# One-hots of the second expert table: sixteen column one-hots on ScalarE as 8-bit tiles, two row one-hots ahead of the last dot products

## The chip, the cores and the metric

The kernel runs on one core of a Trainium2 chip. The metric is the device time of one execution in microseconds (us); a measurement is the median of several executions. Engines are named as the profile names them: PE is TensorE, ACT is ScalarE, DVE is VectorE, POOL is GpSimd and SP is SyncE. POOL and SP mainly issue DMAs here.

## The reference

One layer of a streaming encoder over 384 tokens: 256 prompt tokens (two tiles of 128, "tile 0" and "tile 1") and 128 stream tokens. After an input projection, two attention branches, a gated merge and a residual, a channel mixer (PEER) works on the normalized tokens. The change is in the mixer. Each token picks 16 experts for each of 8 heads out of 128 x 128 = 16384, that is 128 experts a token:

```python
idx  = i * 128 + j                     # top 16 of the sums of two halves' top 16
gate = softmax(best_s)                 # over the 16 of a head
a    = einsum("thkd,td->thk", peer_u[idx], xb)
act  = gelu(a) * gate
out  = einsum("thk,thkd->td", act, peer_v[idx])
```

peer_u and peer_v have 16384 rows of 2048 f32 values. All arithmetic is in f32.

## The kernel before

The two prompt tiles are computed after the stream tokens, at the end of the program, in these stages.

**Dot products.** For each of the 2 x 128 slots (k = 0 to 255) POOL gathers one row of peer_u per token (128 rows of 8 KB) and DVE multiplies and sums it with the tokens (`dot`, L1580). For tile 1 the gathers go round 6 buffers (`ring`); one of them is `spare[:, 0:D]`, another `work[:, 2D:3D]`. A gather waits until the dot that read its buffer before is done. The pick of tile 1's experts is cut into steps and put between the dots, one after each fourth.

**Output, first 1024 columns, by a dense table.** For each tile a table `[i, token, j]` of activations is made and multiplied with all of peer_v's first 1024 columns. The table of a tile is made in 32 groups of 4 tokens (`QUAD` = 4, `QUADS` = 32), numbered g = 0 to 31 for tile 0 and 32 to 63 for tile 1. For each group there are
- a column one-hot `hot_j` (512 columns: 4 tokens x 128), which is 1 where the slot's j equals the column, in `stage`, two slots;
- a row one-hot `hot_i`, the same for i, in `normed`, two slots;
- `hot_a`: the column one-hot times the activation, by ACT (`scaled`, L1144, four instructions), two slots;
- four matmuls `hot_a` x `hot_i` (`scatter`, L867) into one of two PSUM banks;
- the copy of that bank into the table by ACT (`place_table`, L1160).

For tile 0 ACT makes both one-hots itself, as relu(1 - |x - column|) (`distances`, L1124: Abs; `hots`, L1132 and L1134: Relu), beside the dots of tile 1. For tile 1 DVE makes them with a compare (`hots` on DVE, L1599 column, L1600 row) after its last dot. Semaphores: `j_hot`, `i_hot`, `a_hot`, `g_done` and `g_placed` count groups that have passed each step, over both tiles.

**Dense product** (`dense`, L879). Once all 64 groups are placed, PE multiplies both tables with 128 blocks of 128 rows of peer_v. SP loads the blocks (512 KB each, L403) into four buffers: `spare[:, 0:DC]`, `spare[:, DC:2DC]`, `spare[:, 2DC:3DC]` and a part of `work`.

**Output, last 1024 columns, by gathers.** For each of the 256 slots POOL gathers half a row of peer_v per token (4 KB x 128, L571) into one of five buffers and DVE adds it, times the activation, to the sum (`add_half`, L1610). In tile 1's group stage DVE does one add after each group's one-hots, then the rest.

The order on DVE is written out by hand: 256 dots, `prompt_acts(1)`, then for q = 0 to 31 `hots(q)` and `add_half(q)`, then `add_half` 32 to 255, then the sum of the dense part (L1637). The order on ACT: tile 0's groups, `gate_exps(2)`, `place_pair(1)` (tile 1's i and j, transposed, to SBUF), `prompt_gelu(1)`, tile 1's `scaled` and `place_table`. In its loop ACT does `scaled(q + 1)` ahead of `place_table(q)`.

P = 128, D = 2048, DC = 1024, SLOTS = 128.

Of the kernel before, what the change touches and what calls it, by code (L numbers as in the profile page):

```python
# [4 lines left out]

F32 = mybir.dt.float32
U32 = mybir.dt.uint32
ALU = mybir.AluOpType
ACT = mybir.ActivationFunctionType
AX = mybir.AxisListType.X  # L10

P = 128
D = 2048
# [16 lines left out]
SLOTS = PH * TOPK  # L30
# [3 lines left out]
DC = D // 2  # L34
QUAD = 4
QUADS = P // QUAD
UBUF = (8, 6)
# [3 lines left out]
CANDS = TOPK + (TOPK - 1) * FEW  # L41
VBUF = 5
VD = 4

HALVES = ((2, 1, 2, 1, 1), (1, 1, 2, 1, 1), (1, 1, 2, 1, 1), (1, 2, 2, 1, 0))
PICK_HALVES = (0, 1, 1, 0)
# [150 lines left out]
def build(nc, a):  # L197

    with ExitStack() as ctx:
# [11 lines left out]
        spare = sb("spare", [P, 3 * DC])  # L211
# [7 lines left out]
        work = bigr[:, 6 * D:9 * D]  # L219
        stage = sb("stage", [P, 2, CW])  # L220
# [29 lines left out]
        pairT = [fold[:, n * P:(n + 2) * P].rearrange("p (n s) -> p n s", n=2) for n in (6, 18)]  # L250
# [47 lines left out]
        def lay(F, xT, att, y, h, mixed, xn2, prob):  # L298
# [29 lines left out]
                     [rows[:, 2, :], rows[:, 3, :], xTs_flat, yTs[:, :]])  # L328
        ER = Prompt(sem, [spare[:, 0:D], work[:, 2 * D:3 * D]] + ES.urow + ES.vrow + [wflat[:, n, :] for n in range(NP)],
                    [yTr[:, n * DC:(n + 1) * DC] for n in range(4)] + [work[:, 2 * D + DC:3 * D]],  # L330
                    [spare[:, n * DC:(n + 1) * DC] for n in range(3)] + [work[:, 2 * D:2 * D + DC]], ES)
        table = [bigs[:, :].rearrange("p (i t) -> p i t", t=P), bigr[:, 0:8 * D].rearrange("p (i t) -> p i t", t=P)]
        hot_j = stage[:, :, :].rearrange("p b (q n) -> p b q n", q=QUAD)
        hot_i = normed[:, :, :].rearrange("p b (q n) -> p b q n", q=QUAD)
        hot_a = [at[:, 0:2 * CW].rearrange("p (b q n) -> p b q n", b=2, q=QUAD) for at in (xTr_flat, pwork)]

        def ring(k):

            t, n = divmod(k, SLOTS)
            return n % UBUF[0] if t == 0 else (0, 1, 8, 9, 10, 11)[n % UBUF[1]]  # L340

        def landed(k):

            return ER.u_base[ring(k)] + 16 * sum(ring(m) == ring(k) for m in range(k + 1))

        def last_dot(u, end=2 * SLOTS):
            return max(m for m in range(end) if ring(m) == u)
# [4 lines left out]
        @block.sync  # L352
        def _(sp):
            def chunk(n, pieces):

                for s, (w, k0, col) in enumerate(pieces):
                    sp.wait_ge(piece_done, NP * n + s + 1)
                    if not isinstance(n, int):
                        sp.sem_inc(sp_turn, 1)
                    src = w[k0 * P:(k0 + KP) * P, bass.ds(col, CW)].rearrange("(k p) c -> p k c", p=P)  # L360
                    sp.dma_start(wring[:, s, :, :], src).then_inc(w_loaded[s], 16)

            def full(w, col):

                return [(w, KP * s, col) for s in range(NP)]

            sp.dma_start(ln1s[:, :], a["ln1"]).then_inc(S.xT_loaded, 16)
            sp.dma_start(xTs[:, :, :], a["xTs"].rearrange("p (k n) -> p k n", k=KT)).then_inc(S.xT_loaded, 16)
            for F in (S, R):
                c0 = F.chunk0  # L370
                for G in range(2 * GROUPS):
                    br, g = G // GROUPS, G % GROUPS
                    for c in range(3):
                        chunk(c0 + 3 * G + c, full(a["w_in"], (3 * br + c) * WIDTH + g * CW))
                        if F is S and G == 0 and c == 0:
                            sp.dma_start(S.h, a["x"][2 * P:T, :].rearrange("(t p) d -> p t d", p=P)
                                         ).then_inc(S.x_loaded, 16)
                with sp.Fori(0, NCH) as i:
                    n = i * 3 + (c0 + GATES)
                    chunk(n, full(a["w_in"], GCOL + i * CW))  # L380
                    chunk(n + 1, full(a["w_in"], GCOL + D + i * CW))
                    chunk(n + 2, [(a["w_br_a"], 0, i * CW), (a["w_br_a"], KP, i * CW),
                                  (a["w_br_b"], 0, i * CW), (a["w_br_b"], KP, i * CW)])

                sp.wait_ge(F.y_copied, 2 * HEADS)
                sp.wait_ge(F.v_stored, 16 * 2 * GROUPS * F.n)
                sp.dma_start(F.h, a["x"][F.tiles[0] * P:(F.tiles[-1] + 1) * P, :].rearrange("(t p) d -> p t d", p=P)
                             ).then_inc(F.x_again, 16)
                with sp.Fori(0, NCH) as i:
                    chunk(i + (c0 + OUT), full(a["w_out"], i * CW))  # L390
                with sp.Fori(0, NCH) as i:
                    chunk(i + (c0 + PQ), full(a["w_pq"], i * CW))
            sp.wait_ge(ES.v_free, len(ES.vrow) + SLOTS)
            sp.dma_start(a["y"][2 * P:T, :], hs[:, :]).then_inc(y_stored, 16)
            for i in range(P):
                b = i % VD
                if i == 0:
                    sp.wait_ge(ER.u_free, last_dot(0) + 1)
                elif i == 3:
                    sp.wait_ge(ER.u_free, last_dot(1) + 1)  # L400
                elif i >= VD:
                    sp.wait_ge(ER.d_done, i - VD + 1)
                sp.dma_start(ER.dense[b], a["peer_v"][i * P:(i + 1) * P, 0:DC]).then_inc(ER.d_loaded[b], 16)  # L403
            for t in range(2):
                sp.wait_ge(ER.y_summed, 2 * (t + 1))
                sp.wait_ge(ER.v_free, SLOTS * (t + 1))
                sp.dma_start(a["y"][t * P:(t + 1) * P, :], R.h[:, t, :]).then_inc(y_stored, 16)
            sp.wait_ge(y_stored, 16 * TT)
# [484 lines left out]
        def _(act):  # L893
# [216 lines left out]
            def place_pair(t):  # L1110

                act.wait_ge(ER.pair_turned, t + 1)
                act.activation(pairT[t], ps[:, 6, 2 * t * P:(2 * t + 2) * P].rearrange("p (n t) -> p n t", n=2),
                               ACT.Copy).then_inc(ER.pair_placed, 1)
# [22 lines left out]
            def scaled(t, q):  # L1137

                g = QUADS * t + q
                act.wait_ge(ER.j_hot, g + 1)  # L1140
                if t:
                    act.wait_ge(ER.g_done, g - 1)
                for n in range(QUAD):
                    last = act.activation(hot_a[t][:, g % 2, n, :], hot_j[:, g % 2, n, :], ACT.Copy,  # L1144
                                          scale=ractT[:, t, q * QUAD + n:q * QUAD + n + 1])
                last.then_inc(ER.a_hot, 1)

            def prompt_gelu(t):

                act.wait_ge(ER.u_free, SLOTS * (t + 1))  # L1150
                act.activation(rdots[:, t, :], rdots[:, t, :], ACT.Gelu).then_inc(ER.gelu_done, 1)
                act.wait_ge(ER.act_turned, t + 1)
                act.activation(ractT[:, t, :], ps[:, 7, t * P:(t + 1) * P], ACT.Copy).then_inc(ER.act_placed, 1)
                act.wait_ge(ER.act_placed, t + 1)
# [22 lines left out]
                place_table(0, q)  # L1177
            gate_exps(2)
            place_pair(1)
            prompt_gelu(1)  # L1180
            scaled(1, 0)
            for q in range(QUADS):
# [6 lines left out]
        def _(dve):  # L1189
# [393 lines left out]
            def prompt_acts(t):  # L1583

                dve.wait_ge(ER.gelu_done, t + 1)
                dve.tensor_tensor(gates[t], rdots[:, t, :], gates[t], ALU.mult).then_inc(ER.acts_ready, 1)  # L1586

            def hots(q):

                g = QUADS + q  # L1590
                b = g % 2
                grid = iotaP[:, :].unsqueeze(1).to_broadcast([P, QUAD, P])

                def column(n):
                    return pairT[1][:, n, q * QUAD:(q + 1) * QUAD].unsqueeze(2).to_broadcast([P, QUAD, P])

                dve.wait_ge(ER.a_hot, g - 1)
                dve.wait_ge(ER.g_done, g - 1)
                dve.tensor_tensor(hot_j[:, b, :, :], column(1), grid, ALU.is_equal).then_inc(ER.j_hot, 1)  # L1599
                dve.tensor_tensor(hot_i[:, b, :, :], column(0), grid, ALU.is_equal).then_inc(ER.i_hot, 1)  # L1600

            def add_half(k):
# [11 lines left out]
            for k in range(2 * SLOTS):  # L1614
                dot(k)
                if k == SLOTS + 1:
                    finish_first()
                    prompt_acts(0)
                if k % 4 == 3 and len(stages) > 1:
                    stages.pop(0)()  # L1620
            for stage_ in stages:
                stage_()
            prompt_acts(1)
            dve.wait_ge(ER.pair_placed, 2)
            dve.wait_ge(ER.grid_made, 1)
            dve.wait_ge(ER.j_hot, QUADS)
            dve.wait_ge(ER.i_hot, QUADS)
            for q in range(QUADS):
                hots(q)
                add_half(q)  # L1630
            for k in range(QUADS, 2 * SLOTS):
                add_half(k)
# [81 lines left out]
```

## Time and profile before

| | |
|---|---|
| three runs, us | 2847.97, 2853.62, 2841.93 (median 2847.97) |
| the profiled execution, us | 2852.17, of which its span is 2850.3 |
| busy, share of the span | PE 74%, DVE 66%, POOL 43%, ACT 17% |
| DMA | 1047.10 MB, mean 367 GB/s |
| last stages, us from the span's start | dots of tile 1 to 2309.7; groups of tile 1 to 2389.1; dense product to 2830.5; last add to 2842.3 |

How to read it: the page gives busy time of each engine, the chain of waits that ended last, and groups of instructions by line. An instruction's duration includes some overlap with its neighbours on the same engine, so the distance from start to start can be shorter. PE shows two records for each f32 matmul of a group (x8 for four).

### The profile page before, as it was taken

The numbers are of one execution on the slowest core, as the hardware profiler recorded it, in microseconds if no ns is written. First come the engines' busy times: TensorE is split into PE (matmuls) and PEld (weight loads), VectorE is DVE, ScalarE is ACT, GpSimd is POOL, SyncE is SP. The second block draws the span as 40 slices with busy tenths as digits, with TensorE's granted clock in tenths as the row PEclk, the third lists the DMA queues.
The fourth block names the chain that finished last, engine by engine and source line by source line (L and its number), as shares of the span: only waits on it lengthen the run. The fifth ranks groups of instructions, "written<-read, shape, count | busy, mean of one in ns | idle before, by whom it ended". The sixth has DMA issues, their size and how long they took to land.

```text
span 2850.3 us, 19537 instructions
## 1 busy us (share of the span) xinstructions
PE 2110.5 (74%) x6070; PEld 1066.4 (37%) x6070; DVE 1879.8 (66%) x2631; ACT 473.7 (17%) x1107; POOL 1237.0 (43%) x855
## 2 busy tenths in 40 slices
PE   7999999999999998879899920000441048999997
PEld 3665544444545443334344410000331035444443
DVE  1122000296777767657575899999999998666666
ACT  1222100111222210000001000000993043000000
POOL 2000000023444445435443367777777865444444
PEclk9999999999999999999999965555555558999998
DMA  9777688989999999999999999999999988999999
GB/s 360 276 280 259 216 295 287 306 331 367 362 392 397 403 386 373 409 397 392 409 410 357 410 390 403 403 412 377 394 399 416 421 325 288 410 407 405 407 407 358
DMA packets 271464, 1047.10 MB, mean 367 GB/s; under 512 B 19856, under 2 KB 19856, under 8 KB 203280
## 3 DMA queue, kind: packets, MB, share of 16 engines
q0 software_dynamic: 113792, 697.85, 60.9%
q1 hardware_dynamic: 154880, 343.97, 33.2%
q10 hardware_dynamic: 2704, 4.21, 0.4%
q8 instruction: 43, 0.70, 0.1%
q14 instruction: 45, 0.37, 0.0%
HBM read 1036.50 MB, written 9.45 MB: 367 GB/s over the span
## 4 chain that ended last, share of the span: by engine, by line
PE 38%; DVE 26%; DMA 25%; issue 5%; POOL 4%; ACT 1%; SPq 0%; DVEq 0%; POOLq 0%; ACTq 0%
PE ps L590 33%; DMA yTr<-in_peer_v,fold 11%; DVE bigs L1580 7%; DVE bigr L1580 6%; DMA bigr<-in_w_br_a 4%; DVE hr L1610 3%; POOL bigr L561 3%; DMA bigr<-in_w_out 3%; DMA bigr<-in_w_in 2%; DMA bigs<-in_peer_v,idxnow 2%; DVE spare L1580 2%; DMA bigr<-in_peer_v,fold 1%; DVE pwork L1393 1%; PE ps L651 1%; DMA bigs<-in_peer_u,idxnow 1%
## 5 line engine op out<-in xcount | busy, mean ns | idle before, releaser
L590 PE MATMUL ps<-bigr 128*128 128x512 f32 x1920 | 859.3, 605 | 41.1 <-DMA bigr<-in_w_in 22.0
L590 PEld LDWEIGHTS ps<-bigr 128*128 128x128 f32 x1920 | 367.1, 194 | 493.4 <-issue 437.8
L514 POOL DMA_INDIRECT bigs<-in_peer_u,idxnow x128 | 224.9, 1757 | 556.8 <-DVE bigs L1527 537.8
L590 PE MATMUL ps<-bigr,bigs 128*128 128x512 f32 x896 | 408.1, 610 | 20.8 <-DMA bigr<-in_w_in 17.2
L1610 DVE SCALAR_TENSOR_TENSOR hr<-yTr,fold,hr 128x1024 f32<-128x1024 f32 x205 | 263.3, 1284 | 131.5 <-DMA yTr<-in_peer_v,fold 130.1
L1517 DVE SCALAR_TENSOR_TENSOR bigs<-bigs,acts 128x2048 f32<-128x2048 f32 x128 | 300.8, 2350 | 63.1 <-DMA bigs<-in_peer_v,idxnow 63.0
L1527 DVE SCALAR_TENSOR_TENSOR bigs<-bigs 128x2048 f32<-128x2048 f32 x128 | 293.0, 2290 | 67.0 <-DMA bigs<-in_peer_u,idxnow 65.9
L571 POOL DMA_INDIRECT yTr<-in_peer_v,fold x205 | 208.5, 1017 | 220.8 <-DVE hr L1610 212.5
L1580 DVE SCALAR_TENSOR_TENSOR bigr<-bigr 128x2048 f32<-128x2048 f32 x122 | 276.1, 2288 | 6.8 <-DMA bigr<-in_peer_u,fold 6.3
L561 POOL DMA_INDIRECT bigr<-in_peer_u,fold x122 | 238.1, 1952 | 51.3 <-issue 35.5
L590 PEld LDWEIGHTS ps<-bigr,bigs 128*128 128x128 f32 x896 | 171.3, 196 | 220.2 <-issue 213.4
L514 POOL DMA_INDIRECT bigs<-in_peer_v,idxnow x128 | 208.1, 1625 | 51.4 <-issue 39.6
L855 PE MATMUL ps<-ident,fold 128*128 128x128 f32 x2 | 0.9, 474 | 289.7 <-DVE fold L1586 289.7
L1580 DVE SCALAR_TENSOR_TENSOR bigs<-bigs,bigr 128x2048 f32<-128x2048 f32 x96 | 214.8, 2286 | 0.6
L561 POOL DMA_INDIRECT bigs<-in_peer_u,fold x96 | 171.6, 1787 | 62.7 <-issue 25.3
L879 PE MATMUL ps<-spare,bigs 128*128 128x512 f32 x384 | 182.1, 597 | 0.7 <-ACT bigr L1160 0.7
L879 PE MATMUL ps<-spare,bigr 128*128 128x512 f32 x384 | 180.4, 592 | 0.0
L1348 DVE TENSOR_TENSOR bigr<-ps,bigr 128x512 f32<-128x512 f32 x24 | 15.8, 688 | 212.3 <-PE ps L590 212.3
L849 PE MATMUL ps<-ident,fold 128*128 128x128 f32 x4 | 1.4, 448 | 197.0 <-DVE fold L1485 197.0
L867 PE MATMUL ps<-normed,bigr 128*128 128x128 f32 x256 | 65.5, 437 | 101.5 <-issue 93.6
L590 PE MATMUL ps<-bigr,yTr 128*128 128x512 f32 x256 | 117.2, 620 | 17.7 <-DMA bigr<-in_w_br_a 14.5
L500 POOL IOTA fold<- 128x128 f32 x1 | 0.2, 243 | 259.0 <-DVE stage L1372 259.0
(257 smaller groups left out, 2232.4 us busy)
## 6 DMA issues: line engine op xcount, KB each, us to landing
bigr<-in_w_in SPq DMA_DIRECT2D x160, 1024.0 KB, 9.5
spare<-in_peer_v SPq DMA_DIRECT2D x96, 512.0 KB, 6.8
bigr<-in_w_out SPq DMA_DIRECT2D x32, 1024.0 KB, 9.7
bigr<-in_w_pq SPq DMA_DIRECT2D x32, 1024.0 KB, 7.2
bigr<-in_w_br_a SPq DMA_DIRECT2D x16, 1024.0 KB, 9.7
bigr<-in_w_br_b SPq DMA_DIRECT2D x16, 1024.0 KB, 8.1
bigr<-in_peer_v SPq DMA_DIRECT2D x32, 512.0 KB, 6.7
bigr<-in_ckT_a POOLq DMA_DIRECT2D x2, 2048.0 KB, 9.9
```

Source lines behind the costliest of these rows:

```text
L514: pool.indirect_dma_start(row, None, table[:, :], bass.IndirectOffsetOnAxis(ap=col, axis=0)).then_inc(loaded, 16)
L561: pool.indirect_dma_start(ER.urow[u], None, a["peer_u"][:, :], bass.IndirectOffsetOnAxis(ap=eidx[t][:, s:s + 1], axis=0)).then_inc(ER.u_lo ...
L571: pool.indirect_dma_start(ER.vrow[k % VBUF], None, halves, bass.IndirectOffsetOnAxis(ap=hidx[:, t, s:s + 1], axis=0)).then_inc(ER.v_loaded ...
L590: last = mm(ps[:, bank + t, :], src[:, k0 + k, t * P:(t + 1) * P], wring[:, s, k, :], start=(k0 + k == 0), stop=(k0 + k == kt - 1))
L651: last = mm(out[:, b * SQ:(b + 1) * SQ], ckT[:, j, b, :], q_of(j, 0)[:, b * SQ:(b + 1) * SQ], start=(not br and b == 0), stop=True, **sk)
L867: last = mm(ps[:, 4 + b, n * P:(n + 1) * P], hot_a[t][:, b, n, :], hot_i[:, b, n, :], start=(n == 0), stop=True, **sk)
L879: last = mm(ps[:, 2 * t + c, :], table[t][:, i, :], ER.dense[b][:, c * CW:(c + 1) * CW], start=(i == 0), stop=(i == P - 1))
L1393: step(dve.max_index(x[:, lo:lo + 8], v_[:, lo:lo + 8], w))
L1517: dve.scalar_tensor_tensor(h, E.vrow[s], acts[:, s:s + 1], h, ALU.mult, ALU.add).then_inc(E.v_free, 1)
L1527: dve.scalar_tensor_tensor(E.urow[u], E.urow[u], 1.0, xn, ALU.mult, ALU.mult, accum_out=dots[:, s:s + 1]).then_inc(E.u_free, 1)
L1580: dve.scalar_tensor_tensor(ER.urow[u], ER.urow[u], 1.0, R.xn2[:, t, :], ALU.mult, ALU.mult, accum_out=rdots[:, t, s:s + 1]).then_inc(ER.u_ ...
L1610: dve.scalar_tensor_tensor(h, ER.vrow[v], gates[t][:, s:s + 1], h, ALU.mult, ALU.add).then_inc(ER.v_free, 1)
```

## The change

Column one-hots of tile 1's groups 0 to 15 (`EARLY` = 16) are made by ACT, right after `place_pair(1)` and ahead of `prompt_gelu(1)`, as 8-bit values: Abs into the two slots of `hot_i` (f32), then Relu into one of 16 slots of 512 bytes, eight in `stage` and eight in `spare[:, 2DC:]`. For groups 16 to 31 DVE still writes the column one-hots, also as 8-bit, into the eight slots in `stage`, now ahead of its wait for PE. `scaled` of tile 1 reads the 8-bit tiles. The row one-hots of groups 0 and 1 are made by DVE ahead of dot 250 (2 x 128 - 6). The row one-hots of the others stay in the loop. The third and fourth dense buffers change places; the third is waited for as the part of `work` was, the fourth until group 15 has been scaled.

```diff
+EARLY = 16
-                    [spare[:, n * DC:(n + 1) * DC] for n in range(3)] + [work[:, 2 * D:2 * D + DC]], ES)
+                    [spare[:, n * DC:(n + 1) * DC] for n in range(2)] + [work[:, 2 * D:2 * D + DC], spare[:, 2 * DC:]], ES)
+        early_j = [at.bitcast(U8).rearrange("p (b q n) -> p b q n", q=QUAD, n=P)[:, b, :, :]
+                   for at in (stage[:, :, :].rearrange("p b c -> p (b c)"), spare[:, 2 * DC:]) for b in range(EARLY // 2)]
+        def j_slot(q):
+            return early_j[q if q < EARLY else q % (EARLY // 2)]
 # SP, dense loads
+                elif i == 2:
+                    sp.wait_ge(ER.u_free, last_dot(1) + 1)
                 elif i == 3:
-                    sp.wait_ge(ER.u_free, last_dot(1) + 1)
+                    sp.wait_ge(ER.a_hot, QUADS + EARLY)
 # ACT, scaled
+                hot = j_slot(q) if t else hot_j[:, g % 2, :, :]
                 for n in range(QUAD):
-                    last = act.activation(hot_a[t][:, g % 2, n, :], hot_j[:, g % 2, n, :], ACT.Copy,
+                    last = act.activation(hot_a[t][:, g % 2, n, :], hot[:, n, :], ACT.Copy,
+            def early_distances(q):
+                if q >= 2:
+                    act.wait_ge(ER.j_hot, QUADS + q - 1)
+                for n in range(QUAD):
+                    last = act.activation(hot_i[:, q % 2, n, :], iotaP, ACT.Abs, scale=-1.0,
+                                          bias=pairT[1][:, 1, q * QUAD + n:q * QUAD + n + 1])
+                last.then_inc(ER.apart, 1)
+            def early_hot(q):
+                act.wait_ge(ER.apart, QUADS + q + 1)
+                act.activation(early_j[q], hot_i[:, q % 2, :, :], ACT.Relu, scale=-1.0, bias=1.0
+                               ).then_inc(ER.j_hot, 1)
             place_pair(1)
+            act.wait_ge(ER.pair_placed, 2)
+            early_distances(0)
+            for q in range(EARLY):
+                if q + 1 < EARLY:
+                    early_distances(q + 1)
+                early_hot(q)
             prompt_gelu(1)
 # DVE, hots
-                dve.wait_ge(ER.a_hot, g - 1)
+                if q >= EARLY:
+                    dve.wait_ge(ER.a_hot, g - (EARLY if q < EARLY + EARLY // 2 else EARLY // 2) + 1)
+                    dve.tensor_tensor(j_slot(q), column(1), grid, ALU.is_equal).then_inc(ER.j_hot, 1)
                 dve.wait_ge(ER.g_done, g - 1)
-                dve.tensor_tensor(hot_j[:, b, :, :], column(1), grid, ALU.is_equal).then_inc(ER.j_hot, 1)
                 dve.tensor_tensor(hot_i[:, b, :, :], column(0), grid, ALU.is_equal).then_inc(ER.i_hot, 1)
 # DVE, in the loop over the dots
+                if k == 2 * SLOTS - UBUF[1]:
+                    dve.wait_ge(ER.pair_placed, 2)
+                    dve.wait_ge(ER.grid_made, 1)
+                    dve.wait_ge(ER.j_hot, QUADS + EARLY)
+                    dve.wait_ge(ER.i_hot, QUADS)
+                    for q in range(2):
+                        hots(q)
 # DVE, the loop over the groups
             for q in range(QUADS):
-                hots(q)
+                if q >= 2:
+                    hots(q)
                 add_half(q)
```

## Rows read from the trace of the kernel before

**Rows 1.** Chain of waits in order of time: start us, us, what.
```profile
2174.98 6.64 DVE bigr L1580 x6
...
2399.45 10.41 DMA yTr<-in_peer_v,fold
```

**Rows 2.** Stretches: from:to, us, busy (count) by engine, PEclk, DMA share, GB/s.
```profile
2193.00:2310.00 117.00, 0.00 (x0) 0.00 (x0) 109.35 (x97) 1.86 (x3) 100.39 (x47) 0.50 1.01 419
2310.80:2389.10 78.30, 56.56 (x257) 48.95 (x257) 78.19 (x98) 56.71 (x161) 36.75 (x33) 0.65 0.75 241
...
2400.00:2800.00 400.00, 400.00 (x934) 177.10 (x933) 248.98 (x194) 0.00 (x0) 185.52 (x194) 1.00 1.03 407
```

**Rows 3.** Groups by line in 2310.8:2389.1: count | busy us, mean ns | idle before.
```profile
L867 PE MATMUL ps<-normed,pwork 128*128 128x128 f32 x256 | 56.1, 388 | 21.0 <-DVE normed L1600 13.0 <-issue 8.0
...
L1144 ACT ACTIVATE pwork<-stage,fold 128x128 f32<-128x128 f32 x128 | 40.9, 390 | 20.2 <-DVE stage L1599 20.1
L1610 DVE SCALAR_TENSOR_TENSOR hr<-yTr,fold,hr 128x1024 f32<-128x1024 f32 x27 | 34.7, 1284 | 0.1
L571 POOL DMA_INDIRECT yTr<-in_peer_v,fold x26 | 30.5, 1175 | 34.0 <-DVE hr L1610 34.0
```

**Rows 4.** Timeline of the group stage: start us, us, engine, line, operation [idle before].
```profile
2310.84 0.69 DVE L1599 TENSOR_TENSOR stage<-fold 128x512 f32<-128x512 f32 x1
2311.45 0.69 DVE L1600 TENSOR_TENSOR normed<-fold 128x512 f32<-128x512 f32 x1
2311.74 1.28 ACT L1144 ACTIVATE pwork<-stage,fold 128x128 f32<-128x128 f32 x4
2313.11 2.05 PE L867 MATMUL ps<-normed,pwork 128*128 128x128 f32 x8 [1.72 <-DVE normed L1600]
...
2384.95 1.13 PE L867 MATMUL ps<-normed,pwork 128*128 128x128 f32 x8 [1.27 <-DVE normed L1600]
2385.85 0.69 DVE L1600 TENSOR_TENSOR normed<-fold 128x512 f32<-128x512 f32 x1
...
2389.16 3.56 PE L879 MATMUL ps<-spare,bigs 128*128 128x512 f32 x4 [0.69 <-ACT bigr L1160]
```

**Rows 5.** Timeline of ACT: a group of tile 0, then tile 1's first work.
```profile
2006.02 0.57 ACT L1160 ACTIVATE bigs<-ps 128x512 f32<-128x512 f32 x1
2006.49 1.26 ACT L1124 ACTIVATE stage<-fold 128x128 f32<-128x128 f32 x4
2007.66 1.26 ACT L1124 ACTIVATE normed<-fold 128x128 f32<-128x128 f32 x4
...
2009.50 0.61 ACT L1134 ACTIVATE normed<-normed 128x512 f32<-128x512 f32 x1
...
2193.01 0.38 ACT L1113 ACTIVATE fold<-ps 128x256 f32<-128x256 f32 x1 [31.22 <-PE ps L849]
...
2309.80 0.31 ACT L1151 ACTIVATE fold<-fold 128x128 f32<-128x128 f32 x1 [115.11 <-DVE bigr L1580]
```

**Rows 6.** Timeline near the last dots: a dot and a gather's issue.
```profile
2295.02 2.29 DVE L1580 SCALAR_TENSOR_TENSOR bigr<-bigr 128x2048 f32<-128x2048 f32 x1 [0.19 <-DMA bigr<-in_peer_u,fold]
...
2295.94 2.19 POOL L561 DMA_INDIRECT bigr<-in_peer_u,fold  x1 [0.30 <-issue]
```

**Rows 7.** DMA issues, median us to landing, in 2320:2388, 2830:2845 and 2400:2800.
```profile
yTr<-in_peer_v,fold POOLq DMA_INDIRECT x22, 5.2
...
yTr<-in_peer_v,fold POOLq DMA_INDIRECT x4, 6.3
...
yTr<-in_peer_v,fold POOLq DMA_INDIRECT x155, 8.7
```

**Rows 8.** Timeline of the end: last dense matmuls, a gather's issue, the last add.
```profile
2828.60 1.88 PE L879 MATMUL ps<-bigr 128*128 128x512 f32 x4
2828.94 1.08 POOL L571 DMA_INDIRECT yTr<-in_peer_v,fold  x1 [0.31 <-issue]
...
2841.01 1.28 DVE L1610 SCALAR_TENSOR_TENSOR hr<-yTr,fold,hr 128x1024 f32<-128x1024 f32 x1
```

More of the change, by code:

```diff
@@ L7 @@
 U32 = mybir.dt.uint32
+U8 = mybir.dt.uint8
 ALU = mybir.AluOpType
@@ L1623, in _ @@
             prompt_acts(1)
[L1624 to L1627, printed above, removed]
             for q in range(QUADS):
-                hots(q)
+                if q >= 2:
+                    hots(q)
                 add_half(q)
```

## Prediction

> **What bounds the kernel now.** I read the chain of waits in order of time first, because the change touches only the end of the program. Until about 2310 us the chain runs through the dot products on DVE (three in 6.64 us, 2.21 each, where nothing holds them; x6 counts an accumulator read with each) and the gathers that feed them; from 2399 us to the end it is nothing but the gathers of half rows of peer_v into yTr and bigr, each with the add that reads it [rows 1]. Between these lies the stage that the change is about: the 32 groups of the second table (tile 1), from 2310.8 to 2389.1 us.
>
> The table of stretches [rows 2] gives each stage its limit. In 2193 to 2310 DVE is busy 109.35 of 117.00 us and the DMA engines are full (share 1.01), while ACT works 1.86 us and PE nothing. In the group stage of 78.3 us DVE is busy 78.19 us, ACT 56.71, PE 56.56, and the DMA engines carry 241 GB/s at a share of 0.75. From 2400 to 2800 us PE is busy 400.00 of 400.00 us and the DMA engines carry 407 GB/s at 1.03: two limits at once. The dense product ends near 2830.5 us, the adds end at 2842.3 us [rows 8].
>
> So the group stage belongs to DVE. The groups by line [rows 3] show its round: a column one-hot (L1599), a row one-hot (L1600) and one add (L1610). In the timeline the first row one-hot starts at 2311.45 and the last, the 32nd, at 2385.85 [rows 4]: 74.40 / 31 = 2.40 us a round. The first column one-hot starts 0.61 us before the row one-hot and the add takes the rest, so the round is 0.60 + 0.60 + 1.20, starts counted, with no gap. ACT scales a column one-hot in 1.28 us [rows 4] and copies a group out in 0.57 [rows 5]. PE takes 2.05 us for a group at 1.2 GHz and 1.13 us at 2.4 GHz [rows 4]; over the stage the granted clock is 0.65 [rows 2], and the 256 matmuls' 56.1 us [rows 3] are 1.75 us a group.
>
> **The change, part by part.** *16 column one-hots leave DVE.* For groups 0 to 15 DVE no longer writes L1599. Groups 16 to 31 keep it, as an 8-bit write placed ahead of the wait for PE.
>
> *ACT makes them early.* The work is four Abs of 128x128 and one Relu over 512 columns. On tile 0 four Abs take 1.26 us, next start after 1.17, and a Relu 0.61 [rows 5], so a group is about 1.17 + 0.60 = 1.8 us, and 16 of them 28 us. The place is behind place_pair(1), which ends at 2193.39. ACT's next real work is the Gelu at 2309.80, after 115.11 us of idleness [rows 5]. So the work ends near 2222 and 87 us of cover stay. The Gelu's table load moves behind it into the same gap. If this cover were gone, the whole 28 us would stand before the first group. Cost: 0.
>
> *Two row one-hots move ahead of dot 250.* That is 2 x 0.60 = 1.2 us of DVE, plus four waits that have long been met (the last, for ACT, near 2222). Behind it are the last six dots. Gathers for dots 250 to 255 wait only for dots 244 to 249, so no gather is issued later. Near the end a dot waits 0.19 us for its gather, and POOL issues a gather in 2.19 us with 0.30 between two, one each 2.49 us [rows 6]; DVE alone could start one each 2.21 [rows 1]. So 1.2 us of delay are paid off at 0.28 a dot over five gaps (1.4): cost 0, at most 0.3. If DVE had no slack there it would be 1.2.
>
> *The wait of SP.* SP now loads the third dense buffer after the last dot (a step of about 2.5 us) and the fourth only when group 15 has been scaled. Behind that wait on SP's queue stand the dense loads 4 on, and these wait for the first dense matmul anyway. The fourth load comes some 35 us before the stage ends. Cost 0; it even leaves the busy start of the stage.
>
> *The stage itself.* Group 0 isn't sooner: its matmul starts at 2313.11, when ACT's scaling that began at 2311.74 ends (2313.02) [rows 4]. Only DVE is ahead: the adds 0 and 1 are done by about 2313.3. Now row one-hot 2 is the first on DVE in the stage, and it needs group 0 read out of its slot (two slots): 2313.11 + 2.05 + 0.05 = 2315.2, where before it started at 2311.45 + 2 x 2.40 = 2316.25. That is 1.05 us (1.95 were PE at 2.4 GHz by then).
> For groups 2 to 15 DVE needs 0.60 + 1.20 = 1.80 us. The round of the other two engines is next: when group q-2 is done, ACT copies it out (next start after 0.48), scales group q (1.28), PE multiplies (2.05 or 1.13), with about 0.15 us of hand-overs. That is 3.95 us for two groups at 1.2 GHz, 1.98 each, and 3.0, 1.5 each, at 2.4 GHz. With the mean 1.75 it is 1.83. So the pace is 1.80 (PE fast) to 1.98 (PE slow), not 2.40. Over the 13 steps from group 2 to 15 DVE gains 13 x 0.60 = 7.8 or 13 x 0.42 = 5.5.
> Groups 16 to 31 have 0.60 + 0.60 + 1.20 again: 2.40, no gain and no loss, and PE and ACT catch up with DVE within two of them.
> Sum: 1.05 + 5.5 = 6.6 us with PE at 1.2 GHz, 1.05 + 7.8 = 8.9 with PE faster after group 0, 1.95 + 7.8 = 9.8 at the very best. Clock before in the stage is mixed (0.65), so I take 7.8.
>
> The Trainium skill ("TensorE: Matmul & The Clock Gate", Part 1) says that the low clock is the default state and that activity lifts it. By that rule a denser stream of groups stands at the upper end, 8.9 us. The trace agrees that both levels occur in this stage. It doesn't show the denser stream, so the sum above stays between.
>
> *8-bit tiles.* No row of the trace before writes or reads one. The nearest are the same operations on f32: 0.69 us for DVE's one-hot, 1.28 for ACT's four. From below, half of that (0.35) would save 16 x 0.34 = 5.5 us on groups 16 to 31; from above, double (1.38) would cost 16 x 0.69 = 11. I take the f32 rows, because the inputs of DVE's compare stay f32 and the count of elements stays 512.
>
> *What is late next.* The stage ends when the last group is copied out; then the dense product starts and lasts about 441 us, PE full from 2389.16 to 2830.5. The gathers: the stage issues one per round, so 32 before and 32 after. What is left behind it, bytes as well as matmuls, is the same, at the same 407 GB/s. So the gain reaches the end whole, if gathers keep up with 1.8 us. A landing takes 5.2 us in this stage, 6.3 in the tail and 8.7 in the dense stage [rows 7]; in the tail POOL issues one each 1.08 + 0.31 = 1.39 us [rows 8]. Five buffers give (1.28 + 0.1 + 5.2) / 5 = 1.32 us a gather, 2.0 with the 8.7.
>
> **The time.** 7.8 us off the profiled run's 2852.17 (span 2850.3) gives 2844.4. That run lies 4.2 us above the median of the three runs shown. Off the median, 2847.97 - 7.8 = 2840.2 us, and this is my forecast. It is 0.27%, under the 0.5% (14 us) that a measurement of this kernel can tell from no change; the three runs alone spread over 11.7 us.
>
> **Rivals.**
> 1. *The ring of ACT and PE takes DVE's place and PE stays slow*: 1.98 us a group, gain 6.6, 2841.4 us. For it: PE comes from 117 us without work [rows 2], and the mean of 1.75 us lies nearer to 2.05 than to 1.13. Against: groups of 1.13 us occur as well.
> 2. *The gathers hold the adds.* With landings of 8.7 us the pace is 2.0, gain 1.05 + 13 x 0.4 = 6.3. POOL's issue could also grow: 1.18 us in this stage [rows 3], 2.19 beside dots [rows 6]. At 2.19 + 0.30 = 2.49 a gather, the adds of the whole stage would be bound at 2.49 once the five landed rows are used: 27 x 2.49 + 5 x 1.8 = 76 against 77, a gain of about 1, 2847 us. Against: the tail issues one every 1.39 us beside the same adds. The Trainium skill ("SBUF — State Buffer", Who interferes with whom) says that a VectorE instruction with two SBUF inputs contends with a GpSimd instruction that reads SBUF. By that rule a denser DVE lengthens the issue here, at worst to the 2847 us just worked out; the trace shows both lengths beside such instructions.
> 3. *Slower: the 8-bit column one-hots on DVE cost more.* Place: L1599 of groups 16 to 31, on the path with no gap. The point from which it decides is 7.8 / 16 = 0.49 us more each, 1.18 instead of 0.69; at double, 1.38, it is 11 - 7.8 = 3 us slower than before, 2851.
> 4. *The gain isn't passed on*, because the adds end 12 us after the dense product and the DMA engines are full: 2848. Against: the bytes left when the dense product starts don't change, and the engines had room (0.75) before.
> 5. *The change doesn't do what it says*: ACT late. It would need over 115 us for what rows give 28.
>
> **How the numbers follow.** Forecast (a gain of 7 to 10 us) 0.55; rival 1 0.17; rival 2 0.10; rival 4 0.08; rival 3 0.04; rival 5 0.01; a one-hot in half the time (gain 13) 0.05. All but parts of the last and of rival 3 lie within 14 us of before, and the spread of runs moves some across: faster by over 0.5% 0.08, within 0.89, slower 0.03. The range goes from 2840.2 - 9 (the cheap 8-bit one-hot, or the fastest runs) to 2849 (no gain, and the spread): 2831 to 2849.
>
> **What would show it.** ACT busy about 30 us more in 2193 to 2225. Two one-hots of 0.69 just ahead of the sixth last dot, with the first group's scaling within 0.3 us of 2311.7. Row one-hots 1.8 to 2.0 us apart in groups 2 to 15 and 2.4 after. A stage of 70 to 71 us in place of 78.3. The dense product 441 us long, the last add 12 us after it. The forecast is wrong if L1599 with 8-bit output isn't 0.69, if adds wait for yTr within the stage, or if the dense stage grows by what the stage before it lost.

## The result and the profile after

| | before | changed |
|---|---|---|
| first comparison, median of 7 and 7 runs, us | 2852.75 (2833.9 to 2861.2) | 2833.29 (2830.4 to 2838.8) |
| ratio, 95% interval | | 0.9942 (0.9922 to 0.9963) |
| the changed kernel again, median of 12 runs (before: 32), us | 2845.91 (2836.5 to 2861.4) | 2839.81 (2830.2 to 2847.1) |
| ratio, 95% interval | | 0.9970 (0.9952 to 0.9988) |
| profiled execution / span, us | 2852.17 / 2850.3 | 2836.92 / 2835.0 |

The forecast was 2840.2 us, a gain of 7.8. By the ratios the first comparison shows 0.58% (16.5 us) and the second, which the experiments needed, 0.30% (8.5 us); their intervals overlap between 0.9952 and 0.9963. The quotients of the medians are 0.9932 and 0.9979, a sign of how far whole times scatter. The two profiles lie 15.3 us apart. The first task is therefore to find which part of this belongs to the change.

The stretches of the changed kernel that answer to [rows 2] (from:to, length, busy (count) of PE, PEld, DVE, ACT and POOL, PEclk, DMA share, GB/s):

```profile
2187.20:2303.00 115.80, 0.00 (x1) 0.00 (x0) 109.70 (x99) 30.32 (x82) 97.30 (x47) 0.50 1.01 418
2303.00:2373.50 70.50, 48.44 (x257) 41.81 (x257) 68.42 (x85) 55.73 (x162) 47.73 (x33) 0.76 0.81 273
...
2384.00:2784.00 400.00, 400.00 (x934) 177.10 (x933) 248.37 (x194) 0.00 (x0) 189.49 (x194) 1.00 1.02 407
```

ACT now works 30.32 us in the stretch in which it worked 1.86. The group stage, counted from the end of the last dot to the first dense matmul, is 70.5 us; in the kernel before it is 2389.16 - 2309.77 = 79.4. The dense stage is as full as it was.

The same moments in both profiles, us. "Stage" is counted as just said; "tail" is from the start of place_pair(1), which is the last thing ahead of the change, to the end of the last add:

| kernel | place_pair(1) | to last dot's end | stage | first dense matmul to last add | tail |
|---|---|---|---|---|---|
| before | 2193.0 | 116.8 | 79.4 | 453.1 | 649.3 |
| changed | 2187.2 | 115.8 | 70.5 | 453.5 | 639.8 |

Of the 15.3 us, 5.8 had been gained before anything of the change ran. The tail is 9.5 us shorter: 8.9 in the stage, 1.0 in the dots behind place_pair(1), 0.4 given back behind the stage. The 1.0 is no part of the change that I can show: this time is 115.3 to 117.7 us in the ten profiles.

ACT's early work, answering to [rows 5], and the last dots, answering to [rows 6] (timeline: start us, us, engine, line, operation, idle before):

```profile
2187.24 0.38 ACT L1123 ACTIVATE fold<-ps 128x256 f32<-128x256 f32 x1 [31.21 <-PE ps L859]
2187.65 2.44 ACT L1164 ACTIVATE normed<-fold 128x128 f32<-128x128 f32 x8
2190.01 0.61 ACT L1171 ACTIVATE stage<-normed 128x512 uint8<-128x512 f32 x1
2190.65 1.28 ACT L1164 ACTIVATE normed<-fold 128x128 f32<-128x128 f32 x4
2191.84 0.61 ACT L1171 ACTIVATE stage<-normed 128x512 uint8<-128x512 f32 x1
...
2216.79 1.28 ACT L1177 ACT_TABLE_LOAD   x1
...
2288.26 2.29 DVE L1612 SCALAR_TENSOR_TENSOR bigr<-bigr 128x2048 f32<-128x2048 f32 x1 [0.19 <-DMA bigr<-in_peer_u,fold]
...
2290.48 1.29 DVE L1633 TENSOR_TENSOR normed<-fold 128x512 f32<-128x512 f32 x2
2291.69 2.31 DVE L1612 SCALAR_TENSOR_TENSOR bigr<-bigr 128x2048 f32<-128x2048 f32 x1
...
2300.71 2.29 DVE L1612 SCALAR_TENSOR_TENSOR bigr<-bigr 128x2048 f32<-128x2048 f32 x1
2303.04 0.31 ACT L1177 ACTIVATE fold<-fold 128x128 f32<-128x128 f32 x1 [84.97 <-DVE bigr L1612]
```

A group takes 1.83 us (2190.01 to 2191.84), and 85 us of cover are left before the Gelu. The two row one-hots stand behind dot 250, not ahead of it as I had read the loop: `dot(k)` comes first in it, and the block that makes them follows. Five dots follow, from 2291.69 to 2300.71 in four steps, 2.26 us each instead of 2.49. Dot 250 started at 2288.26; at 2.49 us a dot the last would have started at 2288.26 + 5 x 2.49 = 2300.71, and that is when it did. The 1.2 us are paid off in full.

The group stage, answering to [rows 4]; the first line is row one-hot 2 of the kernel before, the rest is the changed kernel:

```profile
2316.25 0.69 DVE L1600 TENSOR_TENSOR normed<-fold 128x512 f32<-128x512 f32 x1
```
```profile
2304.97 2.44 ACT L1155 ACTIVATE pwork<-stage,fold 128x128 f32<-128x128 uint8 x8
2306.35 3.72 PE L877 MATMUL ps<-normed,pwork 128*128 128x128 f32 x16 [1.72 <-issue]
2308.43 0.69 DVE L1633 TENSOR_TENSOR normed<-fold 128x512 f32<-128x512 f32 x1 [1.74 <-PE ps L877]
2309.04 1.28 DVE L1643 SCALAR_TENSOR_TENSOR hr<-yTr,fold,hr 128x1024 f32<-128x1024 f32 x1
2310.24 0.69 DVE L1633 TENSOR_TENSOR normed<-fold 128x512 f32<-128x512 f32 x1
2310.29 1.13 PE L877 MATMUL ps<-normed,pwork 128*128 128x128 f32 x8 [0.22 <-issue]
2311.96 1.13 PE L877 MATMUL ps<-normed,pwork 128*128 128x128 f32 x8 [0.55 <-issue]
...
2331.80 0.70 DVE L1633 TENSOR_TENSOR normed<-fold 128x512 f32<-128x512 f32 x1
2332.40 1.29 DVE L1643 SCALAR_TENSOR_TENSOR hr<-yTr,fold,hr 128x1024 f32<-128x1024 f32 x1
2333.60 0.70 DVE L1631 TENSOR_TENSOR stage<-fold 128x512 uint8<-128x512 f32 x1
2334.20 0.70 DVE L1633 TENSOR_TENSOR normed<-fold 128x512 f32<-128x512 f32 x1
```

Row one-hot 2 starts 2308.43 - 2303.00 = 5.43 us after the last dot's end, where it was 2316.25 - 2309.77 = 6.48: the forecast's 1.05. From there to row one-hot 15 (2331.80) are 13 steps in 23.37 us, 1.80 each. Row one-hot 16 follows after 2.40. DVE's only wait of note is the 1.74 us before row one-hot 2.

### The profile page after: what moved, and what is told of

The parts are those of the page before. It is cut to its first block, busy times and chain, and to the rows that moved or that the text cites. A ratio compares the mean times of both kernels' runs of the same rounds, so it can differ in the third digit from the quotient of the medians.

```text
span 2835.0 us, 19569 instructions
## 1 busy us (share of the span) xinstructions
PE 2098.1 (74%) x6070; PEld 1056.1 (37%) x6070; DVE 1870.1 (66%) x2615; ACT 500.9 (18%) x1187; POOL 1254.9 (44%) x855
## 4 chain that ended last, share of the span: by engine, by line
PE 39%; DVE 25%; DMA 24%; POOL 5%; issue 5%; ACT 1%; POOLq 0%; SPq 0%; DVEq 0%; ACTq 0%
PE ps L600 34%; DMA yTr<-in_peer_v,fold 12%; DVE bigs L1612 7%; DVE bigr L1612 6%; DMA bigr<-in_w_br_a 4%; DVE hr L1643 3%; POOL bigr L571 3%; DMA bigr<-in_w_out 2%; DMA bigs<-in_peer_v,idxnow 2%; DVE spare L1612 2%; DMA bigr<-in_w_in 2%; DVE pwork L1425 1%; PE ps L661 1%; PE ps L718 1%; DVE bigs L1549 1%
## 5 line engine op out<-in xcount | busy, mean ns | idle before, releaser
L524 POOL DMA_INDIRECT bigs<-in_peer_u,idxnow x128 | 230.7, 1802 | 551.1 <-DVE bigs L1559 531.8
L1643 DVE SCALAR_TENSOR_TENSOR hr<-yTr,fold,hr 128x1024 f32<-128x1024 f32 x205 | 263.5, 1286 | 136.8 <-DMA yTr<-in_peer_v,fold 134.4
L1559 DVE SCALAR_TENSOR_TENSOR bigs<-bigs 128x2048 f32<-128x2048 f32 x128 | 293.0, 2290 | 63.8 <-DMA bigs<-in_peer_u,idxnow 62.4
L581 POOL DMA_INDIRECT yTr<-in_peer_v,fold x205 | 219.6, 1071 | 207.0 <-DVE hr L1643 197.6
```

The source lines that it names most:

```text
L524: pool.indirect_dma_start(row, None, table[:, :], bass.IndirectOffsetOnAxis(ap=col, axis=0)).then_inc(loaded, 16)
L581: pool.indirect_dma_start(ER.vrow[k % VBUF], None, halves, bass.IndirectOffsetOnAxis(ap=hidx[:, t, s:s + 1], axis=0)).then_inc(ER.v_loaded ...
L1559: dve.scalar_tensor_tensor(E.urow[u], E.urow[u], 1.0, xn, ALU.mult, ALU.mult, accum_out=dots[:, s:s + 1]).then_inc(E.u_free, 1)
L1643: dve.scalar_tensor_tensor(h, ER.vrow[v], gates[t][:, s:s + 1], h, ALU.mult, ALU.add).then_inc(ER.v_free, 1)
```

## The experiments

All kernels' profiles, in the measure of the table above:

| kernel | ratio (95%) | place_pair(1) | to last dot's end | stage | dense to last add | tail |
|---|---|---|---|---|---|---|
| null_before | 1.0006 (0.9988 to 1.0023) | 2179.4 | 117.7 | 80.3 | 454.4 | 652.4 |
| after_again | 0.9970 (0.9952 to 0.9988) | 2189.5 | 115.3 | 71.1 | 453.6 | 640.0 |
| early31 | 0.9946 (0.9923 to 0.9968) | 2187.7 | 116.1 | 62.4 | 452.3 | 630.8 |
| early8 | 0.9991 (0.9973 to 1.0009) | 2184.0 | 116.4 | 76.3 | 453.7 | 646.4 |
| no_ahead | 0.9980 (0.9963 to 0.9997) | 2192.1 | 116.2 | 70.9 | 451.4 | 638.5 |
| ahead_only | 0.9998 (0.9981 to 1.0014) | 2201.0 | 116.4 | 79.0 | 452.8 | 648.2 |
| no_cover | 1.0059 (1.0038 to 1.0080) | 2185.8 | 116.5 | 100.8 | 455.7 | 673.0 |
| ring_alone | 1.0092 (1.0057 to 1.0126) | 2196.4 | 116.3 | 56.9 | 502.8 | 676.0 |

The ratios of the first four are against 32 runs of the kernel before (median 2845.91 us), those of the last four against 22 others (median 2848.51 us). The last five columns come from one profile each.

### Is the start of the program part of the gain?

> The kernel before, unchanged, against itself. The question: in the pair of profiles shown, place_pair(1) starts 5.8 us earlier in the changed kernel (2187.24 against 2193.01), in code that the change doesn't touch. Theory A, chance: the first 500 us end at another time in each execution; then the ratio here is 1.000 within 0.003, place_pair(1) starts anywhere within some 6 us of 2193, and from it to the end of the last add it is 649.3 us within 1. Theory B, the change moves the start too: place_pair(1) of this kernel stays at 2193 within 1 us.

> The changed kernel, unchanged. From the start of place_pair(1) to the end of the last add 639.8 us within 1 by both theories (649.3 before). Theory A (only the end of the program is faster, by 9.4 us; the rest of the 15 to 19 us is chance): ratio 0.9967, place_pair(1) anywhere within some 6 us of 2190. Theory B (7 us come from ahead of place_pair(1) and belong to the change): ratio 0.994, place_pair(1) within 1 us of 2187.

place_pair(1) in the profiles of null_before and of ahead_only, whose code up to there is the same:

```profile
2179.42 0.38 ACT L1113 ACTIVATE fold<-ps 128x256 f32<-128x256 f32 x1 [31.21 <-PE ps L849]
```
```profile
2201.00 0.38 ACT L1113 ACTIVATE fold<-ps 128x256 f32<-128x256 f32 x1 [31.21 <-PE ps L849]
```

Theory A holds, except for its size. The ten profiles have place_pair(1) anywhere from 2179.4 to 2201.0, a spread of 21.6 us, with no order between kernels; the expected 6 us were too few. The 5.8 us between the first two profiles lie within what identical code shows, so they are put down to chance. They were there long before the change: the same instruction of DVE (L1365, L1397 in the changed kernel) starts at 513.36 us in the first profile and at 507.62 us in the second. The tail is what can be compared from single profiles: 649.3 and 652.4 for the kernel before, 639.8 and 640.0 for the changed one, whose 639.8 had been expected. null_before's 652.4 misses the expected 649.3 within 1: 0.9 of it are in the last dots, 0.9 in the stage and 1.3 behind it. In the stage, PE was at 1.2 GHz in the last group (2.05 us instead of 1.13), and this group ends the stage.

### The number of column one-hots: none, 8, 16, 31

```diff
-EARLY = 16
+EARLY = 31                      # early8: EARLY = 8, slots early_j[q % 16]
 ...
+        early_j += [at.bitcast(U8).rearrange("p (q n) -> p q n", q=QUAD) for at in
+                    [pwork[:, (8 + n) * P:(9 + n) * P] for n in range(3)] + [gates_s[:, :], eidx_s[:, :]]
+                    + [fold[:, n * P:(n + 1) * P] for n in (0, 1, 2, 3, 6, 7, 12, 17, 8, 4)]]
-                    sp.wait_ge(ER.a_hot, QUADS + EARLY)
+                    sp.wait_ge(ER.a_hot, QUADS + 16)       # early8: QUADS + QUADS
 ...
```

In early8 the fourth dense buffer is thus loaded only once the last group has been scaled, since its slots are in use until then; the time from the first dense matmul to the last add (453.7 us) shows no cost of that.

> ACT makes the column one-hots of groups 0 to 30 early (EARLY = 31; the added slots lie in pwork, gates_s, eidx_s and in blocks of fold that are free by then); DVE makes the last. Theory: DVE's round sets the stage, 1.80 us without a column one-hot and 2.40 with. Then groups 2 to 30 go at 1.80 and the stage from the end of the last dot to the first dense matmul, 79.4 us before and 70.5 in the changed kernel, is about 61.6 us; from place_pair(1) to the last add 631 us, ratio to the kernel before 0.9937 if nothing else moves. Rival: PE falls back to 1.2 GHz and the round of ACT and PE takes over, 1.98 us a group: the later groups gain 0.42 each, the stage is 64 us. Second rival: POOL's issue (1.50 us mean in the stage after, 1.94 at times) or the five row buffers hold the adds: DVE waits for yTr within the stage, which is then over 64 us.

> ACT makes only the column one-hots of groups 0 to 7 early (EARLY = 8, sixteen slots as before). Theory: 0.60 us for each column one-hot that leaves DVE from group 2 on and 1.05 for the first two together: the stage is 79.4 - 1.05 - 6 x 0.60 = 74.7 us, ratio about 0.998. Rival: the gain is due to the faster clock of PE or to the slots, not to the number of one-hots; then the stage stays near 70.5 us or near 79.4.

The stage of early31 as one stretch, its groups by line (count | busy, mean ns | idle before), and three steps late in it:

```profile
2303.80:2366.20 62.40, 39.92 (x257) 33.80 (x257) 60.23 (x69) 55.77 (x162) 39.53 (x33) 0.91 0.88 309
```
```profile
L1647 DVE SCALAR_TENSOR_TENSOR hr<-yTr,fold,hr 128x1024 f32<-128x1024 f32 x28 | 35.8, 1277 | 0.3
L585 POOL DMA_INDIRECT yTr<-in_peer_v,fold x26 | 31.7, 1220 | 18.5 <-DVE hr L1647 18.2 <-issue 0.3
L1637 DVE TENSOR_TENSOR normed<-fold 128x512 f32<-128x512 f32 x30 | 20.5, 682 | 1.7 <-PE ps L881 1.7
L1190 ACT ACTIVATE bigr<-ps 128x512 f32<-128x512 f32 x32 | 19.0, 594 | 3.4 <-PE ps L881 2.7
```
```profile
2343.41 0.68 DVE L1637 TENSOR_TENSOR normed<-fold 128x512 f32<-128x512 f32 x1
2344.01 1.28 DVE L1647 SCALAR_TENSOR_TENSOR hr<-yTr,fold,hr 128x1024 f32<-128x1024 f32 x1
2345.20 0.68 DVE L1637 TENSOR_TENSOR normed<-fold 128x512 f32<-128x512 f32 x1
```

DVE keeps 1.80 us a group to the end and waits 1.7 us in all; the adds don't wait for gathers (0.3). The tail is 630.8 us, expected 631. Both rivals fall: granted clock 0.91, not back at 0.50, and no wait for yTr. early8 gave 76.3 us instead of the 74.7 expected. One part is my count: row one-hots 3 to 7 are five steps, not six, so the sum is 79.4 - 1.05 - 5 x 0.60 = 75.35, as the row one-hots of its trace have it (number 8 starts 16.8 us after the last dot's end, 4.05 earlier than before). The other 0.9 are PE's clock in the last group, which ends the stage. The last group and the first dense matmuls of early8, and then of the changed kernel:

```profile
2373.95 2.05 PE L877 MATMUL ps<-normed,pwork 128*128 128x128 f32 x8 [0.35 <-issue]
2376.68 1.98 PE L889 MATMUL ps<-spare,bigs 128*128 128x512 f32 x4 [0.69 <-ACT bigr L1186]
```
```profile
2371.70 1.13 PE L877 MATMUL ps<-normed,pwork 128*128 128x128 f32 x8 [0.36 <-issue]
2373.52 1.98 PE L889 MATMUL ps<-spare,bigs 128*128 128x512 f32 x4 [0.69 <-ACT bigr L1186]
```

2.05 against 1.13 us: 0.92. early31's last group took 2.04 us too, which makes its 61.6 into 62.5 (62.4 measured). The last row one-hot isn't touched by that clock: it starts 76.1 us after the last dot's end before, and 72.0, 67.2 and 58.2 us after it with 8, 16 and 31 early column one-hots. The steps are 4.1 (1.05 + 5 x 0.60 = 4.05), 4.8 (8 x 0.60) and 9.0 (15 x 0.60). So the first three column one-hots are worth 1.05 us together and each later one 0.60 us.

early31 is faster than the kernel before: 2832.37 us, median of 9, against 2845.91, and 2839.81 for the changed kernel in the same comparison. Against the changed kernel the intervals of the ratios overlap, so whole times don't show a gain; the tail (630.8, one profile, against 639.8 and 640.0) does.

### What is the second part, the two row one-hots ahead, worth?

no_ahead is the changed kernel with the block in the loop over the dots taken out; its four waits stand ahead of the loop over the groups:

```diff
 ...
-                if q >= 2:
-                    hots(q)
+                hots(q)
                 add_half(q)
```

> The changed kernel without its second part: the row one-hots of groups 0 and 1 are made in the loop over the groups again, after the last dot. Theory: they were worth nothing. DVE with both in the loop is free 3.6 us after its start (2 x 0.60 + 2 x 1.20), the first group leaves PE 4.4 us after it, and row one-hot 2 waits for that in either kernel. So the stage stays at 70.5 to 71.1 us, and place_pair(1) to the last add at 640 us within 1. Rival: each is worth its 0.60 us, the stage is 1.2 us longer and the last dot 1 us earlier after place_pair(1) than in the changed kernel.

ahead_only is the kernel before with both one-hots of groups 0 and 1 behind dot 249:

```diff
+                if k == 2 * SLOTS - UBUF[1] - 1:
+                    ...                          # the four waits, moved here
+                    for q in range(2):
+                        hots(q)
 ...
             for q in range(QUADS):
-                hots(q)
+                if q >= 2:
+                    hots(q)
                 add_half(q)
```

> The kernel before, with both one-hots of groups 0 and 1 (four of 0.60 us) ahead of dot 250 and nothing early on ACT. Theory: 2.4 us of delay at dot 250, of which 1.4 are paid off before the last dot; row one-hot 2 comes 1.05 us earlier against the last dot; all others at 2.40. Stage about 78.4 us, place_pair(1) to the last add 649.3 within 1, ratio 1.000. Rival: the gain of the change lies in what is ahead of the last dots; then the stage is 4 us or more shorter.

Nothing that shows. no_ahead has a stage of 70.9 us and a tail of 638.5, a little outside the expected 640 within 1 and on the side that speaks against the rival. Its row one-hot 2 starts 5.43 us after the last dot's end, as in the changed kernel: DVE waits for group 0 either way (0.74 us here, 1.74 there). So the first 1.05 us of the gain come from column one-hots, not from the row one-hots.

ahead_only has 79.0 and 648.2, and a ratio of 0.9998. The expectation of 78.4 was 0.6 too low: its row one-hot 2 starts 6.11 us after the last dot's end, 0.4 earlier than before and not 1.05. The order in the code says why. The kernel before waits for group 0 ahead of column one-hot 2, so this one-hot (0.60) stands between the wait and row one-hot 2. The 1.05 us thus need the column one-hots of groups 0, 1 and 2 away from DVE.

### The cover, and the round of ACT and PE

```diff
             place_pair(1)
-            (early work)
             prompt_gelu(1)
+            (early work)
 ...
```

> The changed kernel with ACT's early column one-hots behind the Gelu of tile 1 instead of ahead of it (and the row one-hots in the loop, as in no_ahead, since they would otherwise wait for ever). The cover of the dots is gone. Theory: all of ACT's 16 x 1.83 = 29 us stand before the first group; stage 100 us, place_pair(1) to the last add 669 us, ratio about 1.007. Rival: the gathers that land meanwhile and the dense loads soften it, since the stage isn't full of transfers; it can't, as DVE adds nothing in that time and only five rows and three dense blocks have a buffer: under 660 us would speak for it.

```profile
2302.30:2332.00 29.70, 0.48 (x1) 0.18 (x1) 1.00 (x6) 27.85 (x80) 0.94 (x1) 0.50 0.22 86
```

In these first 29.7 us of no_cover's stage only ACT works and the transfers are at 86 GB/s. The stage is 100.8 us (100 expected), the tail 673.0 (669): all of ACT's work lies in the open once the dots no longer cover it. The rival falls. Of the 4 us too many 2.2 lie behind the stage, where the profiles but ring_alone's scatter from 451.4 to 455.7 us anyway.

ring_alone:

```diff
-                add_half(q)
-            for k in range(QUADS, 2 * SLOTS):
+                if q < 2:
+                    add_half(q)
+            for k in range(2, 2 * SLOTS):
```

> The changed kernel with the adds of slots 2 to 31 moved from the loop over the groups to behind it. It measures the round of ACT and PE alone, which was said to be 1.5 us a group with PE at 2.4 GHz and 1.98 at 1.2 GHz, and whether a shorter stage reaches the end when its gathers don't move along. Theory: DVE has 0.60 or 1.20 us of work a group, so ACT's 0.48 + 1.17 = 1.65 us is the pace of all groups: stage 2.4 + 32 x 1.65 = 56 us, 14 shorter than in the changed kernel. But 30 gathers more are left behind it, and the last add comes later: in the dense product's 440 us some 215 are done, then 39 at 1.39 us are left; last add 495 us after the first dense matmul (453.6 in the changed kernel), 667 us after place_pair(1), slower than both kernels. Rival (the stage alone counts): 626 us.

Stretches of ring_alone: the stage, the dense product, what is left behind it; and two of ACT's rounds:

```profile
2312.70:2369.60 56.90, 38.31 (x257) 32.91 (x257) 36.88 (x55) 53.67 (x162) 5.60 (x4) 0.93 0.19 75
2369.60:2810.00 440.40, 439.73 (x1024) 194.48 (x1024) 276.21 (x216) 0.00 (x0) 212.88 (x216) 1.00 1.02 402
2812.00:2870.00 58.00, 0.00 (x0) 0.00 (x0) 43.43 (x35) 0.00 (x0) 43.03 (x33) 0.50 0.89 307
```
```profile
2329.70 0.59 ACT L1186 ACTIVATE bigr<-ps 128x512 f32<-128x512 f32 x1
2330.18 1.28 ACT L1155 ACTIVATE pwork<-spare,fold 128x128 f32<-128x128 uint8 x4
2331.35 0.60 ACT L1186 ACTIVATE bigr<-ps 128x512 f32<-128x512 f32 x1
```

The round of ACT is 1.65 us (2329.70 to 2331.35), and ACT is the limit: 53.67 of 56.90 us busy. The stage is 56.9 us, 56 expected. Yet the last add comes 502.8 us after the first dense matmul instead of 453.6, and the kernel is slower than both others. The stage moved 75 GB/s instead of 273, and its 30 gathers came due behind the dense product, where 35 adds took 58 us, 1.66 each. I had taken 1.39 each; that explains the 8 us by which 495 was too low (39 x 1.66 = 65, 440 + 65 = 505, against 502.8).

## Why the prediction was right

*What bounds the stage, and by how much each column one-hot shortens it*: right. DVE had no gap at 2.40 us a group and has none at 1.80 (the timeline of the changed kernel), and the last row one-hot of early8, the changed kernel and early31 comes earlier by 0.60 us for each further column one-hot. By the prediction's own count, from the moment 1.08 us behind the last dot at which the first column one-hot used to start, 78.3 us became 69.4, just under its 70 to 71.

*The clock*: the term that was mis-sized. I took 7.8 between 6.6 (PE at 1.2 GHz) and 8.9 (PE faster after group 0); the stage gave 8.9. Group 0 still took 2.05 us, and from group 2 to group 15 PE took 1.13 to 1.16 us a group. The granted clock of the stage is 0.76 against 0.65, and it divides at row one-hot 16 (two stretches of the changed kernel):

```profile
2304.00:2334.00 30.00, 20.18 (x129) 17.22 (x129) 28.14 (x32) 26.73 (x80) 17.98 (x17) 0.90 0.88 315
2334.00:2373.50 39.50, 28.26 (x128) 24.58 (x128) 39.38 (x49) 28.68 (x81) 29.02 (x17) 0.65 0.74 238
```

The rule of the Trainium skill ("TensorE: Matmul & The Clock Gate", Part 1), that activity lifts the clock from its low default, was weighed and not followed; the trace agrees with it here, with 0.90 over the rounds of 1.80 us and 0.65 over those of 2.40. So rival 1 didn't come about. The round of ACT and PE at the high clock was mis-sized as well: I had 1.5 us, half of a chain over two groups, but ACT alone needs 0.48 + 1.17 = 1.65 us for each group, as ring_alone shows. That is still under DVE's 1.80, so the sum isn't touched. In early31 the high clock held through all the groups at 1.80 us.

*The cover*: right; 28 us were estimated, 16 x 1.83 = 29 are in the trace, and no_cover shows their price without it, 100.8 - 70.9 = 29.9 us in the stage against no_ahead, its nearest kernel.

*The two row one-hots*: cost 0, right. But their gain was stated together with that of the column one-hots; no_ahead shows that it is 0. The place was misread by one dot (they stand behind dot 250), with no effect on the sum: 1.2 us were paid off over the five dots that follow.

*The gain passed on whole*: right. 453.1 us from the first dense matmul to the last add before, 453.5 after, 452.3 in early31. The dense product itself takes 439.7 us where 441 were forecast, and the last add ends 13.8 us after it, not 12: the gathers and adds end the program, not PE. ring_alone shows the condition under which it holds: the stage must keep its gathers.

*Gathers and POOL's issue (rival 2)*: the adds didn't wait (0.2 us in all for L1643), though POOL's issue did grow, from 1.18 to 1.50 us in the mean:

```profile
L581 POOL DMA_INDIRECT yTr<-in_peer_v,fold x26 | 38.9, 1497 | 18.6 <-DVE hr L1643 18.3 <-issue 0.3
L1643 DVE SCALAR_TENSOR_TENSOR hr<-yTr,fold,hr 128x1024 f32<-128x1024 f32 x27 | 34.8, 1290 | 0.2
L1155 ACT ACTIVATE pwork<-stage,fold 128x128 f32<-128x128 uint8 x96 | 30.4, 390 | 11.5 <-DVE stage L1631 11.5
...
L1631 DVE TENSOR_TENSOR stage<-fold 128x512 uint8<-128x512 f32 x16 | 11.3, 704 | 0.0
```

The mean hides where. A round of the kernel before, then of the changed kernel a round of 1.80 us and one of 2.40:

```profile
2344.45 0.69 DVE L1599 TENSOR_TENSOR stage<-fold 128x512 f32<-128x512 f32 x1
...
2344.81 1.14 POOL L571 DMA_INDIRECT yTr<-in_peer_v,fold  x1 [1.26 <-DVE hr L1610]
```
```profile
2321.38 1.14 POOL L581 DMA_INDIRECT yTr<-in_peer_v,fold  x1 [0.66 <-DVE hr L1643]
...
2345.59 0.70 DVE L1631 TENSOR_TENSOR stage<-fold 128x512 uint8<-128x512 f32 x1
2345.96 1.75 POOL L581 DMA_INDIRECT yTr<-in_peer_v,fold  x1 [0.66 <-DVE hr L1643]
```

A denser DVE doesn't lengthen the issue here: it takes 1.14 us in the rounds of 1.80 us as in those of 2.40 before, and early31, dense to the end, has a mean of 1.22. The issue takes 1.75 us only in the rounds whose column one-hot DVE writes as 8-bit, at the same distance behind that one-hot (0.37 us) as before (0.36). I had derived the growth from the contention that the Trainium skill describes ("SBUF — State Buffer", Who interferes with whom) between a VectorE instruction with two SBUF inputs and a GpSimd instruction that reads SBUF. The trace doesn't bear this out: the one-hots and adds of the 1.80 us rounds are such instructions too. Why the 8-bit rounds are slower for POOL stays open, and other neighbours lengthen the issue as well (1.93 us at the end of the stage, beside adds alone). The price is hidden here because POOL still waits 0.66 us a round.

*8-bit tiles (rival 3)*: 0.70 us for DVE's 8-bit one-hot where f32 took 0.69, and 390 ns for ACT's scaling of one, as before [rows 3]. The choice of the f32 rows was right for these two engines; POOL's issue beside the 8-bit one-hots, 0.61 us longer, was a cost that the prediction didn't name.

*The size over all*: the forecast of 2840.2 stands against medians of 2833.29 and 2839.81. The first ratio is past the 0.5% to which I had given 0.08; the second is not. The tail says 9.5 us, 0.33%, from the first two profiles, and 9.3 to 12.6 us if either profile of each kernel is taken. What the first comparison has beyond it is of the size of the spread ahead of place_pair(1); no run shows that it comes from there. That the second median lies 0.4 us from the forecast is luck: the kernel before had a median of 2845.91 in that comparison, not 2847.97, and the gain wasn't 7.8. The prediction was off on noise in two ways. It had the spread at 11.7 us from three runs, and the 32 runs of before span 25. And it had 0.5% as the least that a measurement can tell, while both intervals, about 0.2% to either side, lie below 1.

## What to carry to other kernels

Count the round of the engine without gaps, then the round of the next slowest ring, and take work off the first only down to the second: here 2.40, 1.80 and 1.65 us. An idle stretch of another engine is good for it if the results have somewhere to lie, and 8-bit one-hots (512 bytes instead of 2048) are what made room. A stage that is shortened must take its transfers along, or they come due later. For a gain of a third of a per cent, compare one stretch between two fixed moments in several profiles; the whole time hides it in what happens elsewhere.

## What the runs showed of the hardware

- TensorE's granted clock went with the pace of its groups: with starts 2.40 us apart it went to and fro between its levels (0.65 in the mean of the stage before), with 1.80 (early31) the stage's mean was 0.91 and with 1.65 (ring_alone) 0.93. A faster feeding engine thus made the matmuls faster too.
- POOL's issue of the same gather took from 0.93 to 1.94 us in this stage, without any change to it: 1.14 in rounds in which DVE writes f32 one-hots, whether these are 2.40 or 1.80 us long, and 1.75 in those with an 8-bit column one-hot.
- The moment at which untouched code reached the same instruction spread over 21.6 us in ten profiles.
